# Loading the second expert matrix as two half-height transfers with rows of 16 KB

## The chip, the cores and the metric

The kernel runs on one core of one Trainium2 chip. The metric is the device time of one execution in microseconds (us). All data is float32.

## The reference, cut to what matters

One layer of a decoder trunk is computed for 320 tokens (256 of a prompt, 64 of samples) of width 2048. First comes a token mixer (projection `w_in`, a short convolution, a chunked gating MLP and a pooling group, projection `w_out`), then a layer norm, then a mixture of 16 experts of which each token uses 2, all in one group of 4. The change touches only the experts, and of them only the last line:

```python
combine = jnp.sum(jax.nn.one_hot(ids, N_EXPERTS, dtype=jnp.float32) * gates[..., None], axis=1)
hg = jnp.einsum('nd,edf->nef', xt, w_gate)      # w_gate: 16 x 2048 x 512
hu = jnp.einsum('nd,edf->nef', xt, w_up)        # w_up:   16 x 2048 x 512
a = jax.nn.silu(hg) * hu * combine[:, :, None].astype(x.dtype)
out = jnp.einsum('nef,efd->nd', a, w_down)      # w_down: 16 x 512 x 2048
```

The three weight tensors are 201.3 MB together, 67.1 MB of them `w_down`. Every byte is read from HBM once.

## The kernel before

The first 380 us or so are the mixer: `w_in` and `w_out` stream in chunks through SyncE's queue, are split into a high and a low part, and multiplied. Then come the router and the experts.

**Experts.** The 16 experts are walked in order, `e` = 0 to 15, four to a group. Tokens of a group are gathered into `xg` (128 rows of 8 KB, an indirect DMA issued by GpSimd from the DRAM copy `z_rows`), and TensorE picks up to 64 tokens for each expert from them into `xT` (`fill`, L1160, two experts at a time). Per expert TensorE then runs `gate_up` four times (L1200, 16 matmuls each), `combine` of the expert before it (L1187), `down` (two transposes of the activations `a_sb`, L1208, copied by ScalarE to `aT`, L1300, and 32 matmuls, L1218), and ScalarE copies the result out (L1302). After the fourth expert of a group its rows are finished on VectorE and scattered to the outputs by GpSimd.

**Weights.** The weights arrive in units of 2 MB, six for an expert: four of gate and up (`gu_w`), two of down (`down_w`). A ring of 8 slots of 16 KB per partition holds them. SyncE issues everything in order (`sp_experts`): it waits on `ring_used` until TensorE has finished with the unit that lay in the slot, then issues two DMAs of 1 MB for the new unit, both counted on the slot's semaphore `unit_full`, on which TensorE waits before the unit. Nothing else sets the order of the weight stream. SyncE also loads the norm weights (`aln_g`, `aln_b`, `lng`, `lnb`, 1 MB each) between units early on. Before the unit that takes the last slot it waits for the stores `z_stored` (ScalarE's queue, `store_z`, L616), and before the first reuse of a slot for `lgT_made`.

**The contraction of down.** The 512 rows of a down matrix are taken in 4 blocks `f` of 128. In the kernel before, block `f` is rows 128f to 128f + 127, so partition `p` of `down_w[s][:, n, :]` holds row 128(2u + n) + p of `w_down[e]`, u being 0 or 1 for the two down units. One DMA brings one block: 128 partitions, a row of 8 KB each. `a_sb` holds 256 activations per partition: its lower 64 partitions are the 64 tokens of the expert with columns 0 to 255 of the 512, the upper 64 the same tokens with columns 256 to 511. The transpose `c` turns `a_sb[:, 128c:128(c + 1)]`, so that the two halves of its result are the activations for blocks c and 2 + c.

The kernel also has a general path for more than 64 tokens at an expert (`sp_general`, `pe_general`). It isn't run with these inputs.

Of the kernel before, what the change touches and what calls it, by code (L numbers as in the profile page):

```python
# [10 lines left out]
P = 128  # L11
# [26 lines left out]
def hybrid_trunk_kernel(nc, x_prompt, x_sample, state_conv, state_pool, w_in, conv_w, sgu_ln_g,  # L38
# [41 lines left out]
    C = 64  # L80
    HD = D // 2
    HK = KT // 2
    FH = F // 2
    PAIRS = 4
# [12 lines left out]
    def at(name, offset, shape, dt=FP32):  # L97
        return nc.alloc_sbuf_tensor_at(name, shape, dt, offset=base + offset, align_bytes=4)
# [14 lines left out]
    down_w = [at(f"down_w{s}", slot_at[s], [P, 2, D]) for s in range(SLOTS)]  # L113
# [51 lines left out]
    ident = at("ident", CO, [P, P])  # L165
# [30 lines left out]
    a_sb = at("a_sb", G0 + 19 * KB + 512, [P, FH])  # L196
    aT = at("aT", G0 + 20 * KB + 512, [P, FT // 2, 2, C])
    all_silu = at("all_silu", MISC - 16 * KB, [P, F])
    all_act = at("all_act", MISC - 14 * KB, [P, F])
# [45 lines left out]
    ps = nc.alloc_psum_tensor("ps", [P, 8, 512], FP32)  # L245
# [48 lines left out]
    all_rows, all_weights, all_used = S("all_rows"), S("all_weights"), S("all_used")  # L294
# [32 lines left out]
    def wait_alone(eng, sem, value, turns):  # L327


        eng.wait_ge(sem, value)  # L330
        eng.sem_inc(turns, 1)
# [654 lines left out]

    gate_v = w_gate[0].rearrange("e (h p c) f -> p e h c f", h=2, c=HK)
    up_v = w_up[0].rearrange("e (h p c) f -> p e h c f", h=2, c=HK)
    down_v = w_down[0].rearrange("e (j p) d -> p e j d", p=P)
    y_tiles = [y_prompt[0, 0:P, :], y_prompt[0, P:SEQ, :], y_sample.rearrange("b t d -> (b t) d")]  # L990

    ACC, Y, GU, MS, COUNTS = 0, 4, 6, 7, 5
# [19 lines left out]
    def sp_experts(sp):  # L1012
        sp.wait_ge(ylo_ready, 7)
        sp.wait_ge(small_out, 16 * (4 + NB))
        for i in range(UNITS * NE):
            e, u = divmod(i, UNITS)
            s = i % SLOTS
            if i == EARLY:
                sp.wait_ge(w_used, CHUNKS1)
            if i == SLOTS - 1:  # L1020
                sp.wait_ge(lo_ready, CHUNKS1)
                sp.dma_start(aln_g[:, :], ln1_g[0:1, :].to_broadcast([P, D])).then_inc(aln_in, 16)
                sp.dma_start(aln_b[:, :], ln1_b[0:1, :].to_broadcast([P, D])).then_inc(aln_in, 16)
                sp.wait_ge(z_stored, 16 * 6)
                sp.wait_ge(zT_full, 12)
            if i == SLOTS:
                sp.wait_ge(lgT_made, 1)
                sp.dma_start(lng[:, :], ln2_g[0:1, :].to_broadcast([P, D])).then_inc(ln2_in, 16)
                sp.dma_start(lnb[:, :], ln2_b[0:1, :].to_broadcast([P, D])).then_inc(ln2_in, 16)
            if i >= SLOTS:  # L1030
                sp.wait_ge(ring_used, i - SLOTS + 1)
            if u < PAIRS:
                h, c = u // 2, 4 * (u % 2)
                for n, src in enumerate((gate_v, up_v)):
                    sp.dma_start(gu_w[s][:, n, :].rearrange("p (c f) -> p c f", c=4),  # L1035
                                 src[:, e, h, c:c + 4, :]).then_inc(unit_full[s], 16)
            else:
                for n in range(2):
                    sp.dma_start(down_w[s][:, n, :], down_v[:, e, 2 * (u - PAIRS) + n, :])\
                      .then_inc(unit_full[s], 16)  # L1040

    def sp_finish(sp):
# [94 lines left out]
    def pe_experts(pe):  # L1137
# [67 lines left out]
        def down(e):  # L1205
            pe.wait_ge(a_ready, e + 1)
            for c in range(FT // 2):
                last = pe.transpose(ps[:, Y, P * c:P * (c + 1)], a_sb[:, P * c:P * (c + 1)], ident[:, :])  # L1208
            last.then_inc(aT_full, 1)
            pe.wait_ge(aT_ready, e + 1)  # L1210
            for f in range(FT):
                i = UNITS * e + PAIRS + f // 2
                pe.wait_ge(unit_full[i % SLOTS], 32 * (i // SLOTS + 1))
                a = aT[:, f % 2, f // 2, :]
                for q in range(2):
                    for side in range(2):
                        col = HD * side + 512 * q
                        last = pe.matmul(ps[C * side:C * (side + 1), Y + q, :], a,  # L1218
                                         down_w[i % SLOTS][:, f % 2, col:col + 512],
                                         start=(f == 0), stop=(f == FT - 1))  # L1220
                if f % 2:
                    last.then_inc(ring_used, 1)

        info(0)
        for i, (t0, m) in enumerate(TILES):
            last = pe.matmul(ps[:, COUNTS, 0:NE], ones[0:m, :], member[0:m, i, NG:NR],
                             start=(i == 0), stop=(i == 2))
# [255 lines left out]
    def sp_general(sp):  # L1483
        for i, (t0, m) in enumerate(TILES):
            sp.dma_start(tok[0:m, i, :], z_dram[t0:t0 + m, :]).then_inc(all_rows, 16)
        with sp.Fori(0, NE) as e:
            one = bass.ds(e, 1)
            wait_alone(sp, all_used, e + 1, sp_turns)
            for j in range(PAIRS):
                h, c = j // 2, 4 * (j % 2)  # L1490
                for n, src in enumerate((gate_v, up_v)):
                    sp.dma_start(gu_w[WSLOT[j]][:, n, :].rearrange("p (c f) -> p c f", c=4),
                                 src[:, one, h, c:c + 4, :].rearrange("p e c f -> p (e c) f"))\
                      .then_inc(all_weights, 16)
            for f in range(FT):
                sp.dma_start(down_w[WSLOT[PAIRS + f // 2]][:, f % 2, :].rearrange("p (j d) -> p j d", j=1),
                             down_v[:, one, f, :].rearrange("p e d -> p e d")).then_inc(all_weights, 16)
        for i, (t0, m) in enumerate(TILES):
            sp.wait_ge(all_normed, i + 1)
            sp.dma_start(y_tiles[i], tok[0:m, i, :]).then_inc(all_out, 16)  # L1500
        sp.wait_ge(all_out, 16 * 3)

    def pe_general(pe):
        pe.wait_ge(all_x1, 3)
        for i, (t0, m) in enumerate(TILES):
            for q in range(4):
                n = 4 * i + q
                if n >= 2:
                    pe.wait_ge(all_xT, n - 1)
                for t in range(4):  # L1510
                    kt = 4 * q + t
                    col = HD * (kt // HK) + kt % HK
                    last = pe.transpose(ps[:, 2 + n % 2, P * t:P * t + m],
                                        tok[0:m, i, col:HD * (kt // HK + 1):HK], ident[0:m, 0:m])
                last.then_inc(all_xT_full, 1)
        pe.wait_ge(all_xT, 12)
        pe.sem_inc(all_used, 1)
        with pe.Fori(0, NE) as e:
            pe.wait_ge(all_weights, e * (16 * GLOADS) + 16 * GLOADS)
            for i, (t0, m) in enumerate(TILES):  # L1520
                pe.wait_ge(all_a, e * 3 + (i + 1))
                for n in range(2):
                    for kt in range(KT):
                        w = gu_w[WSLOT[kt // 4]][:, n, :].rearrange("p (c f) -> p c f", c=4)
                        last = pe.matmul(ps[0:m, n, :], zT[:, kt, t0:t0 + m], w[:, kt % 4, :],
                                         start=(kt == 0), stop=(kt == KT - 1))
                last.then_inc(all_gu, 1)
                pe.wait_ge(all_a, e * 3 + (i + 2))
                for f in range(FT):
                    last = pe.transpose(ps[:, 2, P * f:P * (f + 1)], all_act[:, P * f:P * (f + 1)], ident[:, :])  # L1530
                last.then_inc(all_aT_full, 1)
                pe.wait_ge(all_aT, e * 3 + (i + 1))
                pe.wait_ge(all_sum, e * 3 + (i + 1))
                for q in range(4):
                    for f in range(FT):
                        last = pe.matmul(ps[0:m, 4 + q, :], all_actT[:, f, 0:m],
                                         down_w[WSLOT[PAIRS + f // 2]][:, f % 2, 512 * q:512 * (q + 1)],
                                         start=(f == 0), stop=(f == FT - 1))
                last.then_inc(all_down, 1)
            pe.wait_ge(all_sum, e * 3 + 4)  # L1540
            pe.sem_inc(all_used, 1)
# [61 lines left out]
    with nc.Block() as block:  # L1603
        @block.sync
        def _(sp):
            sp_program(sp)
            sp_experts(sp)
            overflow(sp, sp_general, sp_finish)
# [13 lines left out]
        @block.tensor  # L1622
        def _(pe):
            pe_mixer(pe)
            pe_router(pe)
            pe_experts(pe)
            overflow(pe, pe_general)
# [40 lines left out]
```

## Time and profile before

| what | us |
|---|---|
| median of 3 runs | 925.8 (924.4 to 926.12) |
| the profiled execution, device time | 922.72 |
| its span from the first to the last instruction | 920.7 |
| TensorE busy | 846.1 |
| VectorE busy | 283.7 |
| ScalarE busy | 223.4 |

The mean granted TensorE clock was 0.978. Moved in all: 271.93 MB. The page gives, for 40 slices of the span, the busy share of each engine, the share in which the 16 DMA engines were busy, and the rate that they moved; its list of DMA issues gives the size and the time from issue to landing of each kind of transfer. In the views of waits a row reads: who waited, for whom, how long in all, how often, longest.

### The profile page before, as it was taken

How to read it: one execution, taken by the hardware profiler on the slowest of the kernel's cores; microseconds unless marked ns; L12 is line 12 of the kernel's file. 1: busy time of each engine (PE TensorE's matmuls, PEld its weight loads, DVE VectorE, ACT ScalarE, POOL GpSimd, SP SyncE). 2: the span in 40 equal slices, each digit the busy share in tenths (PEclk: the TensorE clock that was granted, in tenths of full speed). 3: DMA queues.
4: the chain of work that ended last, by engine and by line, in shares of the span. 5: the costliest groups of instructions: out<-in, count | busy, mean ns of one | idle time of the engine just before them, and what ended most of it. 6: DMA issues, size and time to landing. Idle time of an engine off the chain costs nothing.

```text
span 920.7 us, 11104 instructions
## 1 busy us (share of the span) xinstructions
PE 846.1 (92%) x4695; PEld 580.3 (63%) x4695; DVE 283.7 (31%) x381; ACT 223.4 (24%) x322; POOL 22.8 (2%) x37
## 2 busy tenths in 40 slices
PE   6999999999999999974999999999999899998882
PEld 5989998999999999964353443534435234343220
DVE  5373355335743444341000303102031020220204
ACT  5234313332233323132121220301213012031001
POOL 0000000000001000001000000100001000000000
PEclk9999999999999999985999999999999999999997
DMA  9945433554445546588899999999999999999960
GB/s 289 280 131 161 138 101 120 157 159 152 142 143 158 168 137 254 196 344 355 334 422 420 421 421 422 420 420 420 421 421 421 421 421 421 422 421 421 421 285 30
DMA packets 86201, 271.93 MB, mean 295 GB/s; under 512 B 6089, under 2 KB 58783, under 8 KB 60104
## 3 DMA queue, kind: packets, MB, share of 16 engines
q1 hardware_dynamic: 82858, 262.46, 73.5%
q0 software_dynamic: 1856, 5.28, 1.4%
q10 hardware_dynamic: 1446, 3.59, 1.2%
q8 instruction: 32, 0.52, 0.2%
q14 instruction: 9, 0.07, 0.0%
HBM read 267.23 MB, written 11.54 MB: 303 GB/s over the span
## 4 chain that ended last, share of the span: by engine, by line
PE 79%; DMA 11%; SPq 4%; DVE 3%; ACT 2%; issue 1%; POOLq 0%; POOL 0%; DVEq 0%; ACTq 0%
PE ps L1200 18%; PE ps L433 12%; PE ps L435 12%; PE ps L434 12%; PE ps L1218 10%; DMA gu_w<-in_expert_w_up 9%; PE ps L1160 7%; SPq L1035 3%; PE ps L1187 3%; DMA raw<-in_w_in 1%; DMA xg<-z_rows,row 1%; PE ps L1105 1%; PE ps L455 1%; PE ps L456 1%; ACT aT L1300 1%
## 5 line engine op out<-in xcount | busy, mean ns | idle before, releaser
L1200 PE MATMUL ps<-gu_w,xT 128*64 128x512 f32 x1024 | 230.4, 596 | 16.8 <-DMA gu_w<-in_expert_w_up 16.8
L1200 PEld LDWEIGHTS ps<-gu_w,xT 128*64 128x64 f32 x1024 | 73.1, 137 | 153.0 <-issue 150.4
L433 PE MATMUL ps<-xT_hi,w_hi 128*128 128x320 f32 x512 | 159.3, 311 | 1.8 <-DVE w_lo L607 1.8
L435 PE MATMUL ps<-xT_hi,w_lo 128*128 128x320 f32 x512 | 158.2, 309 | 0.0
L434 PE MATMUL ps<-xT_lo,w_hi 128*128 128x320 f32 x512 | 158.2, 309 | 0.0
L607 DVE TENSOR_TENSOR w_lo<-raw,w_hi 128x2048 fp32r<-128x2048 f32 x50 | 114.1, 2288 | 134.3 <-ACT w_hi L601 134.3
L601 ACT ACTIVATE w_hi<-raw 128x2048 fp32r<-128x2048 f32 x50 | 95.4, 1913 | 139.5 <-PE ps L435 125.8
L1218 PE MATMUL ps<-down_w,aT 128*64 128x512 f32 x512 | 113.4, 595 | 8.2 <-ACT aT L1300 8.2
L1458 DVE TENSOR_TENSOR a_sb<-ps,silu 128x256 f32<-128x256 f32 x16 | 6.8, 424 | 322.5 <-ACT silu L1293 322.5
L433 PEld LDWEIGHTS ps<-xT_hi,w_hi 128*128 128x128 f32 x512 | 96.1, 188 | 2.5 <-DVE w_lo L607 2.0
L434 PEld LDWEIGHTS ps<-xT_lo,w_hi 128*128 128x128 f32 x512 | 96.1, 188 | 0.0
L435 PEld LDWEIGHTS ps<-xT_hi,w_lo 128*128 128x128 f32 x512 | 96.1, 188 | 0.0
L1160 PEld LDWEIGHTS ps<-picked,xg 128*128 128x128 f32 x256 | 63.1, 333 | 33.8 <-issue 22.7
L1218 PEld LDWEIGHTS ps<-down_w,aT 128*64 128x64 f32 x512 | 35.2, 137 | 76.2 <-issue 62.3
L433 PE MATMUL ps<-yT_hi,w_hi 128*128 128x320 f32 x256 | 79.6, 311 | 0.0
L434 PE MATMUL ps<-yT_lo,w_hi 128*128 128x320 f32 x256 | 79.1, 309 | 0.0
L435 PE MATMUL ps<-yT_hi,w_lo 128*128 128x320 f32 x256 | 79.1, 309 | 0.0
L1160 PE MATMUL ps<-picked,xg 128*128 128x128 f32 x256 | 68.7, 416 | 10.9 <-DVE xg L1404 10.9
L1275 ACT ACTIVATE xT<-ps,gbT 128x128 f32<-128x128 f32 x128 | 48.1, 456 | 123.6 <-PE ps L1160 123.6
L433 PEld LDWEIGHTS ps<-yT_hi,w_hi 128*128 128x128 f32 x256 | 48.1, 188 | 0.0
L434 PEld LDWEIGHTS ps<-yT_lo,w_hi 128*128 128x128 f32 x256 | 48.1, 188 | 0.0
L435 PEld LDWEIGHTS ps<-yT_hi,w_lo 128*128 128x128 f32 x256 | 48.1, 188 | 0.0
(215 smaller groups left out, 468.3 us busy)
## 6 DMA issues: line engine op xcount, KB each, us to landing
gu_w<-in_expert_w_gate SPq DMA_DIRECT2D x64, 1024.0 KB, 21.3
gu_w<-in_expert_w_up SPq DMA_DIRECT2D x64, 1024.0 KB, 26.0
down_w<-in_expert_w_down SPq DMA_DIRECT2D x64, 1024.0 KB, 23.6
raw<-in_w_in SPq DMA_DIRECT2D x34, 1024.0 KB, 5.3
raw<-in_w_out SPq DMA_DIRECT2D x16, 1024.0 KB, 5.4
tok<-in_x_prompt SPq DMA_DIRECT2D x2, 1024.0 KB, 6.2
z_rows<-tok ACTq DMA_DIRECT2D x2, 768.0 KB, 4.1
aln_g<-in_ln_g SPq DMA_DIRECT2D x1, 1024.0 KB, 23.6
```

Of the source, the lines that this page charges most:

```text
L433: pe.matmul(out, wh[:, t, col], hi[:, kt, :], start=(n == 0 and t == 0), stop=False)
L434: pe.matmul(out, wh[:, t, col], lo[:, kt, :], start=False, stop=False)
L435: last = pe.matmul(out, wl[:, t, col], hi[:, kt, :], start=False, stop=(n == 1 and t == CK - 1))
L455: pe.matmul(out, wh[:, t, col], hi[:, kt, :], start=(n == 0 and t == 0), stop=False)
L601: act.activation(w_hi[k][:, :], raw[k][:, :], ACT.Copy).then_inc(hi_ready, 1)
L607: dve.tensor_tensor(w_lo[k][:, :], raw[k][:, :], w_hi[k][:, :].bitcast(FP32), ALU.subtract)\
L1035: sp.dma_start(gu_w[s][:, n, :].rearrange("p (c f) -> p c f", c=4), src[:, e, h, c:c + 4, :]).then_inc(unit_full[s], 16)
L1160: last = pe.matmul(ps[:, fill_bank(pair, j), P * c:P * (c + 1)], xg[g % 2][:, col:HD * (j // 2 + 1):HK], picked[:, 2 * two:2 * two + 2, :] ...
L1187: last = pe.matmul(ps[:, ACC + 2 * h + q, :], gatedT[half, k, :], y_sb[half, 512 * q:512 * (q + 1)], start=(k == 0), stop=(k == EG - 1))
L1200: last = pe.matmul(ps[C * side:C * (side + 1), GU, :], x, w[:, :, c, FH * side:FH * (side + 1)], start=(j == 0 and c == 0), stop=(j == PAI ...
L1218: last = pe.matmul(ps[C * side:C * (side + 1), Y + q, :], a, down_w[i % SLOTS][:, f % 2, col:col + 512], start=(f == 0), stop=(f == FT - 1))
L1275: last = act.activation(xT[:, j, c, :], ps[:, fill_bank(pair, j), P * c:P * (c + 1)], ACT.Identity, bias=gbT[:, 1, j // 2, hc:hc + 1], sca ...
```

## The change

The rows of `w_down` are dealt to partitions in another order. Unit `u` of down still is 256 rows of the matrix, but partition `p` now holds the two neighbouring rows 256u + 2p and 256u + 2p + 1, which lie in one run of 16 KB in HBM and land in one run of 16 KB in the slot. The unit still comes in two DMAs of 1 MB on the same semaphore. Before, each of the two covered all 128 partitions with 8 KB a partition; now the first covers partitions 0 to 63 and the second partitions 64 to 127, with 16 KB a partition (`C` is 64, `P` is 128). The transposes take every second column of `a_sb`, so that the activations stand in the same new order. Number, shape and order of the matmuls stay. The general path is changed likewise.

```diff
-    down_v = w_down[0].rearrange("e (j p) d -> p e j d", p=P)
+    down_v = w_down[0].rearrange("e (s p j) d -> p e s j d", s=2, j=2)
@@ sp_experts
             else:
-                for n in range(2):
-                    sp.dma_start(down_w[s][:, n, :], down_v[:, e, 2 * (u - PAIRS) + n, :])\
+                for rows in (slice(0, C), slice(C, P)):
+                    sp.dma_start(down_w[s][rows, :, :].rearrange("p j d -> p (j d)"),
+                                 down_v[rows, e, u - PAIRS, :, :].rearrange("p j d -> p (j d)"))\
                       .then_inc(unit_full[s], 16)
@@ down
             for c in range(FT // 2):
-                last = pe.transpose(ps[:, Y, P * c:P * (c + 1)], a_sb[:, P * c:P * (c + 1)], ident[:, :])
+                last = pe.transpose(ps[:, Y, P * c:P * (c + 1)], a_sb[:, c:FH:2], ident[:, :])
@@ sp_general
-                             down_v[:, one, f, :].rearrange("p e d -> p e d")).then_inc(all_weights, 16)
+                             down_v[:, one, f // 2, f % 2, :].rearrange("p e d -> p e d"))\
+                  .then_inc(all_weights, 16)
@@ pe_general
-                    last = pe.transpose(ps[:, 2, P * f:P * (f + 1)], all_act[:, P * f:P * (f + 1)], ident[:, :])
+                    last = pe.transpose(ps[:, 2, P * f:P * (f + 1)], all_act[:, FH * (f // 2) + f % 2:FH * (f // 2 + 1):2], ident[:, :])
```

On SyncE's queue, at the first expert's last gate and up unit and its two down units, this stood before (a row is the line, the operation, destination and source, partitions x elements, and how many in a row):

```order
 L1035 DMA gu_w_55<-in_expert_w_gate 128x2048
 L1035 DMA gu_w_55<-in_expert_w_up 128x2048
-L1039 DMA down_w_64<-in_expert_w_down 128x2048 x2
-L1039 DMA down_w_65<-in_expert_w_down 128x2048 x2
+L1039 DMA down_w_64<-in_expert_w_down 64x4096 x2
+L1039 DMA down_w_65<-in_expert_w_down 64x4096 x2
 L1035 DMA gu_w_58<-in_expert_w_gate 128x2048
 L1035 DMA gu_w_58<-in_expert_w_up 128x2048
```

Nothing moved: the rows with a plus are the new ones, in the same places, and only their shape differs. On TensorE, around the `down` of expert 1, the order of before is this (names carry their buffer numbers):

```order
L1200 MATMUL ps<-gu_w1_53,xT_137 64x512 x8
L1160 MATMUL ps<-picked_140,xg0_70 128x128 x4
L1187 MATMUL ps<-y_sb_138,gatedT_142 128x512 x4
L1208 MATMUL ps<-ident_115,a_sb_144 128x128 x2
L1218 MATMUL ps<-down_w2_62,aT_145 64x512 x8
L1218 MATMUL ps<-down_w3_63,aT_145 64x512 x8
```

In the changed kernel the same place reads:

```order
L1201 MATMUL ps<-gu_w1_53,xT_137 64x512 x8
L1161 MATMUL ps<-picked_140,xg0_70 128x128 x4
L1188 MATMUL ps<-y_sb_138,gatedT_142 128x512 x4
L1209 MATMUL ps<-ident_115,a_sb_144 128x128 x2
L1219 MATMUL ps<-down_w2_62,aT_145 64x512 x8
L1219 MATMUL ps<-down_w3_63,aT_145 64x512 x8
```

Here too nothing moved; the lines are numbered one higher.

## Rows read from the trace of the kernel before

**Rows 1.** Stretches: length, busy us per engine, granted clock, DMA share, GB/s.

```profile
core 0: us, PE busy (x) PEld busy (x) DVE busy (x) ACT busy (x) POOL busy (x), PEclk, DMA share, GB/s
450.00:870.00 420.00, 400.45 (x1778) 168.44 (x1776) 67.14 (x89) 77.94 (x169) 8.06 (x8) 1.00 1.01 421
```

**Rows 2.** Who waited for whom, over the whole span.

```profile
PE ps L1200 <- DMA gu_w<-in_expert_w_up: 16.8, 16, 1.4
```

**Rows 3.** The chain that ended last, in order of time: start, us, what.

```profile
418.11 10.07 DMA xg<-z_rows,row
...
429.08 7.90 PE ps L1160 x32
436.97 7.02 PE ps L1200 x32
...
797.24 29.21 DMA gu_w<-in_expert_w_up
...
860.29 26.69 DMA gu_w<-in_expert_w_up
887.11 3.65 PE ps L1200 x16
```

**Rows 4.** DMA issues: count, KB each, median us from issue to landing.

```profile
gu_w<-in_expert_w_gate SPq DMA_DIRECT2D x64, 1024.0 KB, 21.3
gu_w<-in_expert_w_up SPq DMA_DIRECT2D x64, 1024.0 KB, 26.0
down_w<-in_expert_w_down SPq DMA_DIRECT2D x64, 1024.0 KB, 23.6
```

**Rows 5.** SyncE's queue at the start: the input's loads, start and us.

```profile
0.82 0.88 SPq L354 DMA_DIRECT2D tok<-in_x_prompt  x2
1.74 0.58 SPq L354 DMA_DIRECT2D tok<-in_x_sample  x1
2.37 9.26 SPq L365 DMA_DIRECT2D raw<-in_w_in  x3
```

**Rows 6.** Stretches in which those loads move.

```profile
3.00:4.00 1.00, 0.00 (x0) 0.00 (x0) 0.25 (x1) 0.00 (x0) 0.00 (x0) 1.00 1.02 401
6.00:7.00 1.00, 1.00 (x6) 1.00 (x7) 0.00 (x0) 0.00 (x0) 0.00 (x0) 1.00 1.02 426
8.00:8.25 0.25, 0.25 (x3) 0.25 (x2) 0.25 (x1) 0.25 (x1) 0.00 (x0) 1.00 0.92 197
8.25:8.50 0.25, 0.25 (x4) 0.25 (x3) 0.17 (x1) 0.23 (x1) 0.00 (x0) 1.00 1.24 262
9.00:9.25 0.25, 0.25 (x3) 0.25 (x2) 0.20 (x1) 0.25 (x1) 0.00 (x0) 1.00 0.81 160
9.50:9.75 0.25, 0.25 (x4) 0.25 (x3) 0.25 (x1) 0.16 (x1) 0.00 (x0) 1.00 1.02 197
15.00:16.00 1.00, 0.00 (x0) 0.00 (x0) 0.00 (x0) 1.00 (x1) 0.00 (x0) 1.00 1.11 350
```

**Rows 7.** Stretches of the first store of z_rows (three DMAs, the third of 64 partitions).

```profile
384.00:384.50 0.50, 0.50 (x5) 0.50 (x5) 0.50 (x1) 0.00 (x0) 0.00 (x0) 1.00 1.02 406
386.00:386.50 0.50, 0.50 (x6) 0.50 (x5) 0.00 (x0) 0.00 (x0) 0.00 (x0) 1.00 1.04 221
386.50:387.00 0.50, 0.50 (x5) 0.50 (x5) 0.00 (x0) 0.00 (x0) 0.00 (x0) 1.00 0.94 209
```

**Rows 8.** The end of the first ring's loads, in stretches.

```profile
430.00:435.00 5.00, 5.00 (x23) 5.00 (x22) 0.00 (x0) 3.01 (x8) 0.00 (x0) 0.71 0.73 301
435.00:440.00 5.00, 5.00 (x25) 2.88 (x26) 0.00 (x0) 4.29 (x9) 0.00 (x0) 1.00 0.01 5
440.00:445.00 5.00, 5.00 (x28) 2.12 (x26) 0.11 (x2) 0.00 (x0) 0.00 (x0) 1.00 0.69 234
```

**Rows 9.** SyncE's queue, first slots taken and first slot reused.

```profile
394.69 2.31 SPq L1039 DMA_DIRECT2D down_w<-in_expert_w_down  x4
...
415.74 0.33 SPq L1035 DMA_DIRECT2D gu_w<-in_expert_w_gate  x1
...
440.60 0.33 SPq L1035 DMA_DIRECT2D gu_w<-in_expert_w_gate  x1
```

**Rows 10.** What SyncE's queue waited for.

```profile
SPq L1035 <- DMA z_rows<-tok: 12.4, 1, 12.4
```

**Rows 11.** The end of the weight stream, in stretches.

```profile
882.00:884.00 2.00, 1.80 (x10) 0.80 (x12) 0.00 (x0) 0.00 (x0) 0.00 (x0) 1.00 0.95 397
886.00:888.00 2.00, 0.89 (x5) 0.40 (x7) 0.00 (x0) 0.00 (x0) 0.00 (x0) 1.00 0.63 266
888.00:890.00 2.00, 2.00 (x12) 0.85 (x10) 0.00 (x0) 0.00 (x0) 0.00 (x0) 1.00 0.52 217
890.00:892.00 2.00, 2.00 (x10) 0.69 (x8) 0.42 (x1) 0.38 (x1) 0.00 (x0) 1.00 0.47 197
```

**Rows 12.** TensorE's weight loads by shape: busy us, mean ns of one, idle before.

```profile
L1208 PEld LDWEIGHTS ps<-ident,a_sb 128*128 128x128 f32 x32 | 3.4, 140 | 9.7 <-issue 9.1 <-DVE a_sb L1458 0.6
L1160 PEld LDWEIGHTS ps<-picked,xg 128*128 128x128 f32 x256 | 63.1, 333 | 33.8 <-issue 22.7 <-DVE xg L1404 11.0
```

## What the change does to the time, predicted

> **What bounds the kernel now.** I read the stretches of the expert stage first. From 450 to 870 us TensorE is busy 400 of 420 us, which looks like the bound, but the DMA share beside it is 1.01 and the rate 421 GB/s [rows 1]: the transfers have no idle time at all. The waits agree: TensorE stood 16.8 us before gate and up for a weight DMA [rows 2]. And the chain that ended last goes late in the stage through weight DMAs that took 29.21 and 26.69 us to land [rows 3]; a transfer of 1 MB (1,048,576 bytes) at 421 GB/s lasts only 2.49 us, so these stood behind some ten others in the queue. The median landing times of 21 to 26 us say the same for all 192 weight transfers [rows 4]. So TensorE and the DMA engines are bound almost equally, at about 28 us of matmuls and 12 x 2.49 = 29.9 us of transfers per expert. Nothing that slows the stream is hidden: it is at once the longer of the two.
>
> **The half-height transfers.** The bytes stay. What is new is a weight DMA of 64 partitions. The trace of before has two DMAs of that height. The first is the load of `x_sample` (512 KB, rows of 8 KB), queued right behind the 2 MB of `x_prompt` on 128 partitions [rows 5]. While `x_prompt` moves, the rate is 401 and 426 GB/s; from about 8.0 us, when those 2 MB are through, it falls to 197, 262, 160 and 197 in the stretches shown, and the mean of the seven quarter microseconds from 8.0 to 9.75 is 199. The DMA share stays at 0.81 to 1.24 [rows 6]. The engines are as busy as before and move half as much. The second is the third part of the first store of `z_rows` (64 partitions, 6 KB each): after the 128-partition parts at 406 GB/s it runs at 221 and 209 GB/s with a share of 1.04 and 0.94 [rows 7]. Load and store show the same: a transfer on 64 partitions keeps all 16 DMA engines busy at half the rate. What limits it then is on the side of the partitions, not of the engines.
>
> The Trainium skill has this as a rule that speaks against the change: "SBUF — State Buffer", section "Door 1: The DMA port swizzle", says that the bandwidth depends on how many of the 16 ports the partitions reach, and that partitions 0 to 63 reach only 8; "DMA: Bandwidth & Descriptors", "Rules for kernel authors", advises one transfer of 128 partitions in place of two on disjoint halves. From the page's 435 GB/s for 16 ports one would estimate 217 for 8, that is 4.8 us for 1 MB. The rows agree.
>
> The price of one: 1 MB takes 4.77 us at 220 GB/s and 5.27 at 199, against 2.49 at 421, so 2.28 to 2.78 us more. I take 2.49, an exact halving, between the load and the store. After the first expert's, 30 down units of two halves are left: 60 x 2.49 = 149.4 us (137 to 167). It holds if the 16 engines work at the same half at the same time, as the queue's order makes them: each has its part of the lower half, then its part of the upper, and so on.
>
> **Engines out of step.** If two engines that would share a way were apart by one half transfer, one would write the lower half while the other writes the upper, and neither would be slowed. The tail of the stream shows that they are not quite in step: the share falls to 0.63, 0.52 and 0.47 from 886 to 892 us, after 0.95 at 882 [rows 11], so about half of the engines had finished some 8 us before the others. At 435 to 440 all were idle (5 GB/s) [rows 8], so the lag starts at nothing and grows. I worked it through for two engines, each with 8 pieces of 2.49 us that touch only its own half, then 4 that alternate lower, upper, lower, upper, with the engine of the upper half ahead: the loss per expert is 10.0 us at no lag (four pieces collide), 5 at a lag of 2.5 us (two do), and again 10 from a lag of 5 us on, since then each engine's foreign pieces meet the other's gate and up. A lag that grows to 8 us passes the cheap place once. If it lies between 0 and 5 us for 6 of the 15 experts at 2.5 us saved on average, that is 15 us back. Ends: 0 (no lag) and 75 (lag 2.5 us throughout). I take 15.
>
> **The first expert.** Its four down DMAs are issued at 394.69, and the first reused slot is loaded at 440.60 [rows 9]. Between them the queue ends at about 434 and lies idle until 440 [rows 8]. Four halves add 4 x 2.49 = 10 us, so it ends at 444: 6.6 us of that are hidden in the idle time and 3.4 show. Two more things can be late. The second store of `z_rows` shares the engines with these transfers and holds SyncE for 12.4 us [rows 10]; the gather of the first group follows and took 10.07 us beside a full queue, and from its landing on all is in the chain [rows 3]. The store was through at 415.7 and the gather issued at 418.1 for another reason, so 2.4 us are spare. If the engines take turns between the queues, each of the store's about 20 pieces per engine waits behind a piece of a down transfer, 8 KB at 26.3 GB/s of one engine (0.31 us) before, 8 to 16 KB at half that (0.6 to 1.2 us) now: 6 to 18 us, of which perhaps half fall before the down transfers end at 421. That makes TensorE's start 0 to 6 us later. I take 5 for the whole term (3 to 9).
>
> **The rest.** Longer rows save what a row costs. Rows of 1 KB (`w_in`) run at 350 GB/s [rows 6], rows of 8 KB at 421: per engine 46.8 ns for 1 KB and 311 for 8 KB, which leaves about 9 ns per row. Of 149 us of down transfers, rows twice as long save 1.5%, 2.2 us, if nothing else changed; under the halving a row's fixed part is hidden, and I count nothing. The transposes read every second column. The same kind of weight load takes 140 ns on contiguous `a_sb` and 333 on `xg` with a step of 8 columns [rows 12], so 32 of them cost between 0 and 32 x 0.19 = 6 us of TensorE. TensorE has over 10 us of idle time per expert once transfers take 39.9 us, so this is hidden; without that cover it would be up to 6. SyncE issues as many DMAs as before.
>
> **The sum.** 149.4 - 15 + 5 = 139.4 us on the profiled execution's 922.7 gives 1062.1. The median of the runs shown is 3.1 us above that execution, so 1065.2.
>
> **The rivals.** *Mostly out of step:* the lag of the engines stays near one half transfer. Loss 75 + 5, so 925.8 + 80 = 1006. For it: the engines are apart in the tail [rows 11]. Against it: the slowest pair of engines sets the time of all, and the lag would have to stay in a window of a few us. Chance 0.15. *The halving doesn't carry over:* the two slow stretches are of single transfers with nothing like them behind; with the upper half queued right behind the lower, engines that are held up on one could be filled by the other, and the stream would stay at 421 GB/s, with rows twice as long. Then the row's fixed part decides: 925.8 - 2.2 = 923.6, a little faster, if the transposes cost nothing; it decides as soon as a down transfer takes less than 2.49 us. Chance 0.09. The same with transposes that cost up to 6 us, or halves that collide only now and then: 926 to 950, chance 0.04.
>
> **How the numbers follow.** Forecast 1065 with chance 0.72: its own ends are 925.8 + 137 - 25 + 3 = 1041 and 925.8 + 167 + 9 = 1102. The range for 8 in 10 reaches down to the first rival and leaves out the second: 1000 to 1103. This kernel can be told from no change at about 0.2%, 1.9 us. Faster by more than that needs the second rival at its best: 0.05. Within it: 0.05. Slower: 0.90.
>
> **What would show it.** In the changed kernel's profile the stretch from 450 us on should show a DMA share still near 1, and a mean rate of about 421 x 29.9 / 39 = 320 GB/s in place of 421; in stretches of 2 us it should swing between about 420 (gate and up) and 215 (down), if the engines are in step, and hang in between, near 320, if not. TensorE should wait some 10 us per expert on a weight DMA, mostly at the down units and the gate and up units behind them, where 16.8 us in all stood before. The transposes should stay near 140 ns per weight load. I am wrong if the rate stays at 421 through the down transfers (second rival) or if TensorE's waits for DMAs come to about 5 us per expert (first rival).

## The result and the profile after

The changed kernel takes 1206.05 us, the kernel before 925.2 us beside it (medians of 6 runs each). The ratio is 1.296, with a 95% interval of 1.292 to 1.301. Two of the six runs of the changed kernel (1218.3 and 1220.92 us) were in a slower state of the chip and are left out of the ratio, as such runs are in all ratios below; the other four have a median of 1198.7 us. The direction was forecast, and the size was not: 139 us more were predicted, and measured were 281 by the medians, 274 by the ratio. 1206 lies outside the range of 1000 to 1103.

The page of the changed kernel, with a span of 1202.2 us: what each engine was busy, and the 40 slices (the clock and the DMA share in tenths, then GB/s).

```profile
PE 938.1 (78%) x4695; PEld 610.2 (51%) x4695; DVE 283.9 (24%) x381; ACT 224.1 (19%) x322; POOL 22.6 (2%) x37
...
PEclk8999999999999859989889777867888797888877
DMA  9554255444447789999999999999989979897940
GB/s 299 166 161 139 77 180 162 147 140 151 147 150 292 207 329 263 328 246 293 327 295 285 317 279 220 292 192 277 254 236 278 205 285 257 239 325 171 307 103 28
```

The engines that move the bytes are nearly as busy as before (a share of 0.99 to 1.01 up to 900 us, then 0.89), and the rate is down from a flat 421 GB/s [rows 1] to between 171 and 329. Stretches of the changed kernel: four in a row, two at a high rate and two at a low one in turn, and the wider ones of 200 us.

```profile
core 0: us, PE busy (x) PEld busy (x) DVE busy (x) ACT busy (x) POOL busy (x), PEclk, DMA share, GB/s
709.00:725.00 16.00, 10.66 (x39) 4.30 (x40) 0.00 (x0) 1.01 (x1) 0.00 (x0) 0.79 1.01 407
725.00:757.00 32.00, 23.98 (x83) 11.67 (x82) 0.42 (x1) 6.39 (x17) 0.00 (x0) 0.79 1.01 184
757.00:774.00 17.00, 9.94 (x36) 3.33 (x36) 0.00 (x0) 0.37 (x1) 0.00 (x0) 0.80 1.01 392
774.00:808.00 34.00, 16.48 (x56) 5.47 (x52) 0.46 (x4) 1.01 (x1) 0.00 (x0) 0.74 1.01 186
500.00:700.00 200.00, 152.67 (x594) 59.80 (x592) 22.54 (x32) 23.75 (x50) 3.06 (x3) 0.87 1.01 296
700.00:900.00 200.00, 125.41 (x432) 50.49 (x429) 19.31 (x28) 21.97 (x47) 3.01 (x3) 0.80 0.99 252
900.00:1100.00 200.00, 138.99 (x492) 54.53 (x492) 17.86 (x21) 22.35 (x48) 1.99 (x2) 0.83 0.89 253
```

From 700 us on, an expert consists of a fast phase of some 16 us near 400 GB/s and a slow one of 32 us at about 185. I had forecast 20 and 20 us at 420 and 215. The slow phase carries 32 x 0.184 = 5.9 MB, though the halves of one expert are only 4.2 MB: gate and up units move in it too, at the slow rate.

The waits of the changed kernel answer to [rows 2], and its chain, at the start of the experts, to [rows 3].

```profile
PE ps L1201 <- DMA gu_w<-in_expert_w_up: 122.8, 34, 8.6
...
PE ps L1219 <- DMA down_w<-in_expert_w_down: 81.1, 23, 7.5
```

```profile
408.46 21.28 DMA z_rows<-tok
...
430.59 9.87 DMA xg<-z_rows,row
...
441.35 7.90 PE ps L1161 x32
449.25 3.15 PE ps L1201 x13
```

TensorE waits 204 us for weights where it had waited 16.8. The store of `z_rows` has come into the chain with 21.28 us: the first matmul of the experts starts at 449.25 instead of 436.97, 12.3 us later. Of these, 2.6 us were there before any half-height transfer moved: the first down DMA is issued at 397.32 instead of 394.69, and in the kernels of the experiments, which share the stage before it, at 394.3 to 396.1. So 9.7 us of this trace belong to the change.

The two profiled executions are 1204.07 - 922.72 = 281 us apart, and this splits as follows, with numbers from the experiments below. The late start is 12.3 us. Halving alone, all engines in step, costs 39.9 - 29.9 = 10 us per expert, 150 us for 15; 39.9 is the prediction's figure, and the transfers measured alone take 39.3 (e5_lag) to 40.1 (12.58 MB at the 314 GB/s of e1_stream). SyncE's first down DMA of an expert is issued at 460.75 for expert 1 and at 1130.38 for expert 15, 47.8 us per expert (before: 448.48 and 862.46, 29.6 us), so 7.9 us per expert, 118 us, are lost on top. Together 280. The last part is a remainder here; what it is, the experiments have to show. It is what the prediction lacked.

### The profile page after: what moved, and what is told of

It reads as the page before. It is cut to its first block, busy times and chain, and to the rows that moved or that the text cites. A ratio compares the mean times of both kernels' runs of the same rounds, so it can differ in the third digit from the quotient of the medians.

```text
span 1202.2 us, 11104 instructions
## 1 busy us (share of the span) xinstructions
PE 938.1 (78%) x4695; PEld 610.2 (51%) x4695; DVE 283.9 (24%) x381; ACT 224.1 (19%) x322; POOL 22.6 (2%) x37
## 4 chain that ended last, share of the span: by engine, by line
PE 51%; DMA 36%; another core or an unknown queue 5%; SPq 3%; DVE 2%; ACT 1%; issue 1%; POOLq 0%; POOL 0%; ACTq 0%; DVEq 0%
DMA down_w<-in_expert_w_down 22%; DMA gu_w<-in_expert_w_up 11%; PE ps L1201 10%; PE ps L433 9%; PE ps L435 9%; PE ps L434 9%; PE ps L1219 6%; PE ps L1161 2%; DMA z_rows<-tok 2%; SPq L1039 2%; SPq L1035 1%; DMA xg<-z_rows,row 1%; PE ps L1188 1%; PE ps L481 1%
## 5 line engine op out<-in xcount | busy, mean ns | idle before, releaser
L1201 PE MATMUL ps<-gu_w,xT 128*64 128x512 f32 x1024 | 278.7, 697 | 122.8 <-DMA gu_w<-in_expert_w_up 122.8
L1201 PEld LDWEIGHTS ps<-gu_w,xT 128*64 128x64 f32 x1024 | 87.5, 160 | 293.6 <-issue 291.8
L1219 PE MATMUL ps<-down_w,aT 128*64 128x512 f32 x512 | 149.9, 741 | 84.3 <-DMA down_w<-in_expert_w_down 81.1
L1219 PEld LDWEIGHTS ps<-down_w,aT 128*64 128x64 f32 x512 | 44.0, 169 | 178.6 <-issue 95.7
L1303 ACT COPY y_sb<-ps 128x1024 f32<-128x1024 f32 x16 | 16.2, 1012 | 227.7 <-PE ps L1219 227.7
L1294 ACT ACTIVATE silu<-ps 128x256 f32<-128x256 f32 x16 | 6.1, 384 | 254.4 <-PE ps L1201 254.4
```

Source lines behind the costliest of these rows:

```text
L1201: last = pe.matmul(ps[C * side:C * (side + 1), GU, :], x, w[:, :, c, FH * side:FH * (side + 1)], start=(j == 0 and c == 0), stop=(j == PAI ...
L1219: last = pe.matmul(ps[C * side:C * (side + 1), Y + q, :], a, down_w[i % SLOTS][:, f % 2, col:col + 512], start=(f == 0), stop=(f == FT - 1))
L1303: act.copy(y_sb[:, :].rearrange("p (b c) -> p b c", b=2), ps[:, Y:Y + 2, :]).then_inc(y_ready, 1)
```

## The experiments

### Height, row length and order, one at a time

**e2_halves8** takes the kernel before and changes only the height.

```diff
-                for n in range(2):
-                    sp.dma_start(down_w[s][:, n, :], down_v[:, e, 2 * (u - PAIRS) + n, :])\
+                for rows in (slice(0, C), slice(C, P)):
+                    sp.dma_start(down_w[s][rows, :, :],
+                                 down_v[rows, e, 2 * (u - PAIRS):2 * (u - PAIRS) + 2, :])\
```

> The kernel before with one edit: each down unit still comes in two DMAs of 1 MB, but each covers 64 partitions with two separate rows of 8 KB (old order of the contraction, transposes as before). Theory H: the time of the changed kernel, 1190 to 1220 us. Rival L (rows of 16 KB): 925.

Measured: 1220.1 us (1199.6 to 1245.5, 4 runs), the profiled run 1216.5 where that of the changed kernel took 1204.1. The rows are 8 KB, the order and the transposes are the old ones, and the whole loss is there.

**e3_neworder8** takes the changed kernel and gives the height back.

```diff
-                for rows in (slice(0, C), slice(C, P)):
-                    sp.dma_start(down_w[s][rows, :, :].rearrange("p j d -> p (j d)"),
-                                 down_v[rows, e, u - PAIRS, :, :].rearrange("p j d -> p (j d)"))\
+                for n in range(2):
+                    sp.dma_start(down_w[s][:, n, :], down_v[:, e, u - PAIRS, n, :])\
```

> The changed kernel with the new order of the contraction and the strided transposes, but each down DMA covers all 128 partitions with one row of 8 KB. Theory H: 925 to 931 us (the transposes cost at most 6). Rival L or a cost of the order itself: clearly above 931.

Measured: 925.47 us, ratio 1.0004 (0.9987 to 1.002). The order of the contraction costs nothing. Its transposes do take longer, in the groups by shape of this kernel 205 ns for a weight load instead of 140 [rows 12]; 32 x 65 ns = 2.1 us of TensorE, hidden.

```profile
L1208 PEld LDWEIGHTS ps<-ident,a_sb 128*128 128x128 f32 x32 | 5.0, 205 | 9.7 <-issue 9.1 <-DVE a_sb L1458 0.6
```

**e4_full16** keeps the rows of 16 KB and brings each down unit in one DMA of 2 MB over 128 partitions.

```diff
-                for rows in (slice(0, C), slice(C, P)):
...
+                sp.dma_start(down_w[s][:, :, :].rearrange("p j d -> p (j d)"),
+                             down_v[:, e, u - PAIRS, :, :].rearrange("p j d -> p (j d)"))\
+                  .then_inc(unit_full[s], 16)
```

TensorE's waits on `unit_full` count 16 for such a unit in place of 32.

> The changed kernel with each down unit in one DMA of 2 MB over 128 partitions with rows of 16 KB (the order and the transposes of the change; half-height transfers gone). Theory H: 922 to 928, a little faster than before if long rows save their fixed part (2.2 us) and later landings of whole units cost nothing. Rival L: over 1000.

Measured: 921.81 us, ratio 0.997 (0.9951 to 0.9988), 3.6 us less than the kernel before. Long rows and half as many down DMAs are worth this together, near the little that was reckoned for the rows (2.2 us); the two were not taken apart. The stretch from 450 to 870 us moves 423 GB/s instead of 421.

```profile
450.00:870.00 420.00, 402.44 (x1784) 170.32 (x1782) 67.13 (x89) 77.94 (x169) 8.47 (x9) 1.00 1.01 423
```

This version beats both kernels, the one before by 0.3%. It is the change's idea without the split by partitions.

### The transfers alone

**e1_stream** has nothing but weight transfers on SyncE's queue, in a ring of 8 slots.

> Weight transfers alone: everything but the weight loads is left out (no mixer, no matmuls, outputs unwritten), so no engine holds the stream back. Eight sections of 24 or 36 units of 2 MB: gate loads; down loads as before (128 partitions x 8 KB); 128 partitions x 16 KB in one DMA; the two halves of the change; halves with two rows of 8 KB from the old order; only the lower half; six experts of 4 gate units + 2 down units in halves; the same with full-height rows of 16 KB. Theory H (height halves the rate): sections 1 to 3 at 421 GB/s or a little above, sections 4 to 6 alike at 199 to 220 GB/s, the mixed section at about 421 x 29.9 / 39.9 = 315, the last at 421. Rival L (long rows are slow): section 3 and the last are slow too, section 5 is at 421. Rival M (the mixture of heights is what is slow, engines out of step collide with full-height transfers): sections 4 to 6 near 210, but the mixed section clearly under 315, near the 265 GB/s that the changed kernel shows per expert (12.58 MB in 47.4 us).

In the order of the sections, gate units, down as before, full height with 16 KB, halves with 16 KB, halves with 8 KB, the lower half only, the mixture of the change, and the mixture with full-height rows of 16 KB:

```profile
4.00:100.00 96.00, 0.00 (x0) 1.00 1.01 423
126.00:222.00 96.00, 0.00 (x0) 1.00 1.01 422
250.00:340.00 90.00, 0.00 (x0) 1.00 1.01 429
370.00:560.00 190.00, 0.00 (x0) 1.00 1.01 211
610.00:800.00 190.00, 0.00 (x0) 1.00 1.01 212
850.00:930.00 80.00, 0.00 (x0) 1.00 1.01 205
980.00:1170.00 190.00, 0.00 (x0) 1.00 1.01 314
1220.00:1370.00 150.00, 0.00 (x0) 1.00 1.01 424
```

The exact halving and the 315 GB/s of the mixture are as predicted. So the price per transfer was right, and the mixture alone does not give the 252 to 296 GB/s of the kernel. Something that the bare stream has not must be there in the kernel.

### The lag between the DMA engines

**e5_lag** puts half of the DMA engines behind by a copy that only 8 of the 16 carry. The lag is counted in pieces, 8 KB for each of these engines.

```diff
+                sp.dma_start(scratch[:, 0:lag, :], w_gate[0].rearrange("(a b) k f -> a b (k f)", a=8)
+                             [:, 0, 0:lag * D].rearrange("a (m d) -> a m d", d=D)).then_inc(lagged, 16)
```

> Weight transfers alone again (everything else of the layer is left out). Eight sections of six experts (4 gate units on 128 partitions, 2 down units in halves of 64 partitions x 16 KB), each begun with a copy from HBM to HBM of 8 rows, which 8 of the 16 DMA engines carry, so that these start late by some multiple of 8 KB: 0, 4, 8, 16, 24 pieces (about 0, 1.2, 2.5, 5, 7.5 us if a piece costs 0.31 us), then three with the upper half first, at 4, 8, 16 pieces. Theory K (what the two-engine reckoning of the prediction says: engines only share, nothing is lost beyond it): 315 GB/s at no lag, 336, 361, 315, 315 in the sections behind it, and up to 421 in one of the last three. Theory S (an engine that is out of step collides with the full-height transfers at more than the price of sharing): about 315 at no lag and 250 to 265 GB/s at the long lags, with stretches at 140, as the changed kernel shows from 700 us on.

The same six experts (four gate units and two down units in halves each), now with 0, 4, 8, 16 and 24 pieces of lag, and with the upper half first and 4, 8 and 16 pieces:

```profile
10.00:230.00 220.00, 0.00 (x0) 1.00 1.01 318
260.00:480.00 220.00, 0.00 (x0) 1.00 1.01 298
530.00:750.00 220.00, 0.00 (x0) 1.00 1.01 272
820.00:1060.00 240.00, 0.00 (x0) 1.00 1.01 258
1130.00:1390.00 260.00, 0.00 (x0) 1.00 1.01 232
1440.00:1640.00 200.00, 0.00 (x0) 1.00 1.01 312
1690.00:1890.00 200.00, 0.00 (x0) 1.00 1.01 306
1950.00:2190.00 240.00, 0.00 (x0) 1.00 1.01 266
```

At 8 pieces, about 2.5 us, the prediction's reckoning promised 361 GB/s, and 272 were measured. A lag never helps. It costs more the longer it is, and between 16 and 24 pieces the rate passes through the kernel's 252. From the issue times of gate units four experts apart an expert takes 39.3 us at no lag, 45.6 at 8 pieces, 48.9 at 16 and 55.6 at 24. The slow phase grows with the lag and falls below a third of the full rate; with 24 pieces it lasts from about 1167 to 1212 us, where 20 us of halves are in an expert:

```profile
1160.00:1165.00 5.00, 0.00 (x0) 1.00 1.01 418
...
1170.00:1175.00 5.00, 0.00 (x0) 1.00 0.97 136
...
1205.00:1210.00 5.00, 0.00 (x0) 1.00 0.94 134
```

**e10_lag2** asks where a lag costs. Its edit is another list of sections.

> Weight transfers alone (everything else is left out), eight sections: gate units only with half of the engines 24 pieces behind; halves only, 0, 8 and 24 pieces behind; lower half only, 24 behind; four experts of gate units and full-height 16 KB rows, 24 behind; four experts of 4 gate units and 2 lower halves (1 MB each), 24 and 0 behind. If a lag costs only where heights are mixed: sections without halves at 421 to 428 whatever the lag, halves alone at about 211 or above whatever the lag, and the mixed one with lower halves clearly slower with the lag than without. If a lag costs anywhere: gate units alone fall below 421 too. If lagging engines alternate the halves to advantage (the prediction's reckoning): halves alone with 8 pieces of lag rise well above 211.

Gate units with 24 pieces of lag ran at 422 GB/s, full-height rows of 16 KB mixed with them at 425, halves alone at 210, 213 and 213 with 0, 8 and 24 pieces, the lower half alone at 206. The gate units also show the size of the lag: the section ends with a DMA share of 0.50 to 0.58 from 124 to 130 us, half of the engines at work for some 6 us more. Four gate units and two lower halves ran at 259 with the lag and 350 without. The first row is the end of the halves alone with 24 pieces:

```profile
858.00:860.00 2.00, 0.00 (x0) 1.00 0.53 115
...
1010.00:1110.00 100.00, 0.00 (x0) 1.00 1.01 425
1140.00:1290.00 150.00, 0.00 (x0) 1.00 1.00 259
1310.00:1420.00 110.00, 0.00 (x0) 1.00 1.02 350
```

So a lag costs only where the two heights are mixed. Halves alone gain nothing from it either. With 24 pieces the two groups of engines were still apart at the end by about one half transfer (5 us): the share is 0.44, 0.53 and 0.39 from 856 to 862 us. So they must have been on different halves for much of the time, and the rate stayed at 213. The advantage that two engines on different halves were to have doesn't show.

**e12_twoq** makes the mixture permanent, with two queues.

> Weight transfers alone (everything else is left out), now on two queues at once, SyncE's and ScalarE's, each with 24 units and six slots of its own, so that each DMA engine has both kinds in front of it all the time. Sections: gate units beside full-height units with 16 KB rows (101 MB); gate units beside halves (101 MB); gate units beside lower halves (75 MB); lower halves beside upper halves (50 MB); lower beside lower (50 MB). If what limits is only how many engines write to one side of the partitions at a moment: the fourth section reaches about 421 GB/s (120 us), the fifth 211 (240 us), and the second comes near 421 too, since both sides get the same bytes. If a half-height transfer holds its DMA engine at half speed whatever the others do: the fourth stays at 211 (240 us) and the second at 101 MB in 360 us = 280. If mixing heights itself is harmful: the second and third fall below 280.

Gate units beside full height; gate units beside halves; gate units beside lower halves; lower beside upper; lower beside lower:

```profile
20.00:220.00 200.00, 0.00 (x0) 1.00 1.01 425
260.00:560.00 300.00, 0.00 (x0) 1.00 1.01 228
...
660.00:780.00 120.00, 0.00 (x0) 1.00 1.01 219
...
920.00:1120.00 200.00, 0.00 (x0) 1.00 1.01 223
1170.00:1370.00 200.00, 0.00 (x0) 1.00 1.01 205
```

Two more rows, of the stretch from 260 to 560 us, give what each queue moved there (packets, MB, share of the engines' time); q10 has the halves, q1 the gate units:

```profile
q10 hardware_dynamic: 3353, 43.94, 64.4%
q1 hardware_dynamic: 3357, 24.38, 36.5%
```

Both simple theories fall. Lower beside upper covers all 128 partitions and still moves 223 GB/s, where 421 were expected if only the number of engines on one side counts. (If all engines were on the same half at each moment here, that would say little; e10_lag2, with 213 for halves at 24 pieces of lag, speaks against that way out.) And gate units beside halves move 228. The 280 that was named beforehand for "each kind keeps its own rate" holds for equal bytes of both, and in this stretch 64% of the bytes are halves: 24.38 MB at 422 and 43.94 MB at 211 GB/s take 266 us, which makes 257 GB/s. 228 is still less. What is slowed can be read from the two rows: the gate units had 36.5% of the engines' 300 us and moved 24.38 MB in it, at 223 GB/s instead of 422, and the halves ran at 227. A full-height transfer beside half-height ones runs at their pace. That would explain the phases: traffic is slow for as long as some engines have a half-height transfer in front of them. In step this is 20 us of an expert; with a lag the halves begin on the leading engines and end on the last, and gate units before and behind them are drawn in.

**e8_instep** removes the lag in the kernel itself.

```diff
+            if i > PAIRS and u == PAIRS:
+                sp.wait_ge(unit_full[(i - 1) % SLOTS], 32 * ((i - 1) // SLOTS + 1))
```

> The changed kernel with one more wait on SyncE: from expert 1 on, before an expert's first down unit is issued, the last gate and up unit must have landed, so that all 16 DMA engines are idle for a moment and start the halves together. If the lag between engines is what costs more than the halving (40.3 us per expert in step, 44 to 56 with a lag, in the transfers measured alone): 15 experts at about 40.3 + 2 to 4 us for the drained queue in place of 47 to 50, so 1090 to 1140 us instead of 1206, although the wait itself can only cost time. If the lag doesn't matter in the kernel: 1230 to 1265, slower by the drained queue.

Measured: 1137.48 us (1135.36 to 1139.03), ratio 1.2299 (1.2269 to 1.2329). A wait that does nothing but drain the queue once per expert makes the kernel 61 us faster by the ratios, 68 us between the profiled executions (1204.07 and 1136.2). One expert of it:

```profile
755.00:773.00 18.00, 14.50 (x60) 5.34 (x62) 0.46 (x4) 1.01 (x1) 0.00 (x0) 0.90 1.01 420
773.00:775.00 2.00, 2.00 (x12) 0.69 (x8) 0.00 (x0) 0.00 (x0) 0.00 (x0) 1.00 0.71 295
775.00:777.00 2.00, 0.72 (x4) 0.23 (x4) 0.00 (x0) 0.00 (x0) 0.00 (x0) 1.00 0.03 12
777.00:779.00 2.00, 2.00 (x12) 0.86 (x10) 0.00 (x0) 0.00 (x0) 0.00 (x0) 1.00 0.67 164
...
777.00:797.00 20.00, 11.37 (x46) 4.02 (x42) 8.06 (x12) 1.25 (x3) 0.00 (x0) 0.83 0.98 210
```

From 755 to 773 it is at full rate, then the gap of the drained queue, then about 20 us of halves. By the shares the gap is (0.29 + 0.97 + 0.33) x 2 = 3.2 us of idle engines. The first down DMAs of experts 1 and 15 are issued at 465.16 and 1086.53, 44.4 us per expert; twelve of the fourteen intervals lie between 42.4 and 44.9 us, which is 39.9 in step and 3.2 for the gap, and two are 50.5 and 48.7, which no run explains. The 68 us gained and the 15 x 3.2 = 48 us that the gaps cost make 116 us that came from the lag, where the account above left 118. The course fits too: from 500, 700 and 900 us on, each for 200 us, the changed kernel moves 296, 252 and 253 GB/s, so its loss grows, and this one 281, 288 and 292. The lag is shown as the cause of that part.

**e6_balanced** asks whether the uneven row gathers make the lag. It replaces them, and likewise the scatters of the finished rows, by plain transfers spread evenly over 128 partitions, and leaves out which tokens reach which expert.

```diff
-            pool.indirect_dma_start(
-                out=xg[g % 2][:, :], out_offset=None, in_=z_dram,
...
+            pool.dma_start(xg[g % 2][:, 0:1280], z_dram[0:P, 0:1280]).then_inc(gathered, 16)
```

> The changed kernel, with the gathers and scatters of the token rows replaced by plain transfers of about as many bytes spread evenly over 128 partitions (columns 0 to 1279 of 128 rows in, two times 128 rows of 2 KB out per group; which tokens reach which expert is left out, the work per expert is the same). If the uneven row transfers put half of the DMA engines behind and that is what costs more than the halving: the stretches from 600 us on rise from 254 towards 315 GB/s, and the time falls from 1206 towards 1090. If the engines fall out of step by themselves or by the order of the queue: 1190 to 1220 as before.

Measured: 1177.5 us (1172.6 to 1205.9), ratio 1.2719 (1.2664 to 1.2773). From 700 to 900 us the rate is 265 instead of 252. By the ratios the time falls by 23 us. Some 4 of them are an earlier start (the experts' first matmul is at 444.91 instead of 449.25); per expert, 46.0 us instead of 47.8 are left between issues. So the uneven row transfers are a small part, some 20 to 28 us of the 118, and the engines also fall out of step in another way, which no run settles.

### TensorE's clock

The granted clock of the changed kernel falls to 0.50 (1.2 GHz) in stretches in which TensorE waits for weights (it is 0.50 from 733 to 734 us, where TensorE does nothing and the rate is 213 GB/s), and its mean is 0.881. That could release slots later. **e9_warm4** and **e11_warm2** put matmuls with zero weights ahead of every unit.

```diff
+            for n in range(WARM):
+                pe.matmul(ps[0:C, GU, :], zero64[:, :], lng[:, 512 * (n % 4):512 * (n % 4) + 512],
+                          start=opens, stop=opens)
```

> The changed kernel with 4 more matmuls (zero weights) on TensorE ahead of each unit from expert 1 on; one such matmul took 593 ns of busy time with 12 of them per unit, so 4 are about 2.4 us, 14 us per expert, which fits into the idle 19 us. If the fallen clock costs time: granted clock near 1.0 and 20 to 60 us less than 1206. If the transfers alone set it: 1190 to 1230.

Measured: 1221.4 us, ratio 1.3198 (1.317 to 1.3226), inconclusive. I had sized the matmuls wrongly: with 20.6 us of them per expert TensorE was busy 99 of 100 us and was the bound again. (With 12 in place of 4, in **e7_warm**, it came to 1840.5 us.)

> The changed kernel, with 12 more matmuls (zero weights, so the sums stay) on TensorE ahead of each unit from expert 1 on, about 2.6 us of work each, so that TensorE idles less and keeps its clock. If the fallen clock (0.5 granted in the gaps) delays the release of slots and so starves the DMA engines (share 0.88 from 900 to 1100 us): granted clock near 1.0, DMA share back to 1.0 and 20 to 60 us less. If the transfers alone set the time: 1190 to 1230, unchanged.

> The changed kernel with half the filling of e9: 2 more matmuls with zero weights ahead of each unit from expert 1 on. In e9 the 4 were recorded as 8 matmuls at a point, 3.4 us, 20.6 us per expert, so that TensorE (28.4 + 20.6 = 49 us per expert) became the bound itself and e9 says nothing of the clock. Two make 10.3 us, 38.7 us per expert, well under the 47.8 us that an expert takes. If the fallen clock costs time: granted clock near 1.0, DMA share back near 1.0 and 20 to 60 us less than 1206. If the transfers alone set the time: 1190 to 1225.

Measured with two: ratio 1.2987 (1.2894 to 1.308), against the changed kernel's 1.2963. The mean clock rises from 0.88 to 0.94 (in the trace kept, of a run of 1218.4 us), and from 900 to 1100 us the DMA share is 0.90 and the rate 255, as without them:

```profile
900.00:1100.00 200.00, 166.00 (x588) 67.99 (x586) 17.87 (x21) 22.35 (x48) 1.99 (x2) 0.93 0.90 255
```

The interval leaves room for about 1% either way; the 20 to 60 us that the fallen clock was to explain are not in it as a gain of more than 7 us. The test is not complete: the clock came back only in part, and the added matmuls take 10.3 us of TensorE per expert themselves. But e5_lag shows the same slow phases with no matmul at all. The fallen clock goes with the waits for slow transfers and is not their cause.

## Why the prediction was right and wrong

**The bound.** Right. The stream was the longer of the two, so its slowing showed in full; TensorE's waits grew from 16.8 to 204 us.

**The price of a half-height transfer.** Right: 2.49 us more for 1 MB was taken, and 211 GB/s in e1_stream gives 1,048,576 bytes in 4.97 us, 2.48 more. The rule that was cited from the Trainium skill, "SBUF — State Buffer", section "Door 1: The DMA port swizzle", agrees in size with this: the estimate from its figures was 217 GB/s. What a lower and an upper half in flight together move was measured here: 223 GB/s.

**Engines out of step.** This is the step that failed, and the miss is almost wholly in it. It was booked as a gain of 15 us with 0 and 75 as its ends, both on the side of gain (the forecast's own lower end then counts 25, without a reason); measured is a loss of 116 to 118. The reckoning let two engines share a way and lose nothing else, and concluded that an engine on the other half is undisturbed and a gate unit beside it too. e5_lag, e10_lag2 and e12_twoq refute both. A sign against it was in the trace of before. I averaged the load of `x_sample` from 8.0 to 9.75 us and left out what follows, where the full-height chunks of `w_in` already moved behind it:

```profile
9.75:10.00 0.25, 0.25 (x5) 0.25 (x4) 0.25 (x1) 0.25 (x1) 0.00 (x0) 1.00 0.67 119
10.00:10.25 0.25, 0.25 (x4) 0.25 (x4) 0.09 (x2) 0.25 (x2) 0.00 (x0) 1.00 0.91 152
10.25:10.50 0.25, 0.25 (x5) 0.25 (x3) 0.25 (x1) 0.25 (x1) 0.00 (x0) 1.00 1.15 156
10.50:10.75 0.25, 0.25 (x5) 0.25 (x4) 0.25 (x1) 0.25 (x2) 0.00 (x0) 1.00 1.11 139
```

These are 119 to 156 GB/s, from 10.00 on at a share of 0.91 to 1.15, where the chunks alone run at 350 and the half-height load at 199. TensorE gets `x_sample` only at 11.8 us, so its load had not landed in these stretches. The mixture was slower than either of its parts, in plain sight, though four quarters of a microsecond are little evidence. Had it been priced as a loss, with a lag that may reach 8 us [rows 11], the upper end would have lain higher; how near to the result, I have not worked out.

**The first expert.** Sized too small: 5 us taken (3 to 9), 12.3 measured, of which 9.7 belong to the change. The store of `z_rows` ran 21.28 us instead of at most 11.5, 10 us more; this is the "6 to 18 us later" of which half was counted. It may be the same mixture, a store beside halves; no run takes it apart.

**The rest.** Right. Rows of 16 KB raise 422 to 429 GB/s at full height, 1.7%, where 1.5% was reckoned, and under the halving they bring nothing (211 against 212), as was taken. The transposes cost 2.1 us of TensorE, inside 0 to 6, hidden.

**The rivals.** The first (out of step, 1006) had the right place and the wrong sign. The second (no halving) and the third (halves that collide only now and then) were refuted by e1_stream.

**What was to show it.** A rate near 320 was named, with swings between 420 and 215. The swings are there, the mean is 252 to 296, and the slow phase is lower and longer than named. TensorE's waits for weights came to 12.8 us per expert instead of 10.

## What to carry to other kernels

Keep every DMA of a saturated stream on all 128 partitions; if rows are to be longer, lengthen the DMA and do not split the partitions. Here a few half-height transfers slowed down what moved beside them, so count the time during which any engine still has one in front of it, not the bytes in them. When a rare slow stretch in a trace is all the evidence there is, read its tail too, since that is where it meets the next transfer.

## What the runs showed of the hardware

On one queue, a stream that mixes heights depends on how well the 16 DMA engines keep in step: 318 GB/s in step and 232 with 24 pieces of lag, with the same transfers in the same order. A stream of one height doesn't care (422 and 425 GB/s with a lag, 213 for halves). For that reason a wait that drains the queue made a transfer-bound kernel faster. Beside halves on another queue, full-height transfers move at 223 GB/s instead of 422. Why a full-height transfer falls to the pace of half-height ones beside it, and why the rate falls to 134 GB/s, below both 211 and 421, stays open: these runs show when it happens, not what is shared.
